# Two matmuls at once in half the array: memory attention's scores by pairs of heads, and the forget gate's 16-row products

## The chip, the cores and the metric

The kernel runs on one core of one Trainium2 chip. The metric is the device time of one execution in microseconds (us). The runs before the change gave a median of 926.34 us (three runs, 926.17 to 926.77). The profiled execution is one of its own: 927.06 us, of which the span from the first to the last instruction is 924.4.

## The reference

The model has two layers; the change is in the first. A tile of 256 tokens (`x`, 256 x 1024) goes through a wide projection, then three branches are gated and added, then a feed-forward part, then a second layer (state space and dilated attention). All is float32. The two places that the change touches are these:

```python
# the forget gate of gated linear attention: 16 columns of the projection, then a 16 x 512 matrix
log_a = log_sigmoid(a_gla @ w_gla_gate + b_gla_gate) / 16.0        # a_gla 256 x 16, w_gla_gate 16 x 512

# memory attention: 4 heads, keys of 64, values of 256; 256 tokens against 256 rows of a memory
s_m = einsum('bshd,bmhd->bhsm', q_m, k_m) * (MEM_DQK ** -0.5)       # MEM_DQK = 64
p_m = softmax(s_m, axis=-1)
o_mem = einsum('bhsm,bmhd->bshd', p_m, v_m)
```

Beside memory attention stands gated linear attention: its decayed products between tokens of a chunk are made level by level (nine levels, from the diagonal up).

## The kernel before

Each engine has its own program, written out by hand in one order, and the engines meet at semaphores. Weights stream from memory through a ring of three slots. A projection of 1024 x 1024 is a "group": seven block products of 128x512 blocks (numbered 1 to 7, in an order such as 1, 5, 2, 7, 3, 6, 4) in place of eight. Sums of weight blocks and of row blocks (`group_t1`, `t3`, `t2`, `t4`, `group_rows`) and the sums of the results (`group_z`, `group_v`, `group_last`) are made by VectorE; a full sum of weights (128x2048) is a long operation there. Product 5 waits for t1, 7 for t3, 6 for t2, 4 for t4 and z. In the text (GT,2) is product 2 of group GT. The groups around the change are MV (the memory's values), GT and GU (two gates).

A float32 matmul shows as two LDWEIGHTS and two MATMUL records.

**The forget gate.** ScalarE copies the 16 gate columns of both token tiles out of PSUM into `a_tok` (line 796). TensorE turns them (`turn("ga", ...)`), ScalarE copies the result into rows 0 to 15 of `aT`, and the job "gg" (lines 2249 to 2251) multiplies `wgate[0:16]` and `aT[0:16]` for the four heads in turn, right before the job "q2".

**Memory attention and the levels** share a stage of nine steps, i = 0 to 8 (TensorE from line 2526, ScalarE from line 927, VectorE from line 1599). In each step TensorE does, in this order: one or two or more products of a group; the scores of head i (i < 4); the transposes of the probabilities of head i - 1 (1 <= i <= 4), which wait for ScalarE's exponentials; the values of head i - 2 (2 <= i < 6); the products of level i. The scores of a head are two products of 128x256 over all 128 rows. Two heads share 128 rows (64 each), so for an even head the keys in `kmT[0]` have zeros in rows 64 to 127, and for an odd head those in `kmT[1]` have zeros in rows 0 to 63; GpSimd sets these zeros (lines 609 to 611), and ScalarE's `turned_keys` copies the keys in two pieces of 64 rows (line 717).

**What sets the order.** Scores, values, levels and the final outputs are "units". They use two PSUM banks in turn (`bank["score"]`). TensorE's `unit("score")` takes the next bank and first waits until the unit two before it has been taken out:

```python
if kind == "score" and n - 2 in BY_ACT:
    pe.wait_ge(sem("score_copied"), BY_ACT.index(n - 2) + 1)
elif n >= 2:
    pe.wait_ge(sem(kind + "_taken"), by_dve(n - 1) if kind == "score" else n - 1)
```

Scores and most levels are taken out by VectorE (a head by two reductions with the maximum, line 1473, called from line 1620 on), values and the levels 1, 2 and 8 by ScalarE. `linear_units` (line 84) lists the order: S0 L0 S1 L1 S2 V0 L2 S3 V1 L3 V2 L4 V3 L5 and so on. Before it takes the scores of step 0, VectorE makes `group_t1(GT)`; in step 2 it makes `group_t4(GT)` and `group_z(GT)` first. Before VectorE multiplies the operands of level 2 it waits until TensorE is done with level 1 (`if i in (1, 2, 8)`), since they use the same buffers.

All elementwise operations of VectorE between two tensors show as line 1176, all products of groups as line 2382 or 2378, all jobs as line 2297.

Of the kernel before, what the change touches and what calls it, by code (L numbers as in the profile page):

```python
# [83 lines left out]
def linear_units():  # L84

    units = []
    for i in range(9):
        units += [("scores", i)] * (i < EH) + [("values", i - 2)] * (2 <= i < EH + 2) + [("level", i)]
    return units + [("out", n) for n in range(4)]
# [68 lines left out]
for _job in JOBS:  # L158
# [43 lines left out]
    "kpe_rows": "rotated key, twice", "key_zero": "GpSimd: zeros beside the rotated key, then beside the memory's keys", "q_rows": "queries without rotation", "qpe_rows": "rotated queries",  # L202
# [69 lines left out]
def build(nc, d, out):  # L272
    with ExitStack() as ctx:
# [23 lines left out]
        a_tok = sb("a_tok", [P, TT * GR])  # L297
# [37 lines left out]
        kmT, qmT = (qpT[:, 0:512], kpeT), qpT[:, 512:1024]  # L335
# [19 lines left out]
        adiag = a1(256)  # L355
# [157 lines left out]
        def _(sp):  # L513
            def constants_of_rows():
# [9 lines left out]
                sp.dma_start(wgate[0:GR, :], d["w_gla_gate"][0]).then_inc(sem("consts_in"), 16)  # L524
# [46 lines left out]
        def _(pool):  # L571
# [9 lines left out]
            for name in list(COLS)[1:]:  # L581
                a, n = COLS[name]
                pool.dma_start(prow[a:a + n, :], d[name].rearrange("o (a b) -> (o a) b", b=P)).then_inc(sem("rows_in"), 16)
            pool.memset(kpeT[64:128, 0:SEQ], 0.0).then_inc(sem("key_zero"), 1)
# [21 lines left out]
            for n, i in enumerate(GATES):  # L606
                if n == 2:
                    pool.wait_ge(sem("mla_scores"), MH)
                    pool.memset(kmT[0][64:128, :], 0.0).then_inc(sem("key_zero"), 1)
                    pool.memset(kmT[1][0:64, 0:SEQ], 0.0).then_inc(sem("key_zero"), 1)  # L610
                    pool.wait_ge(sem("key_zero"), 4)
                    pool.wait_ge(sem("group_product"), product_at(MV, 6))
                    pool.memset(amat, 0.0).then_inc(sem("amat_zero"), 1)
# [51 lines left out]
        def _(act):  # L665
# [124 lines left out]
            ck = ckv.rearrange("p (t c) -> p t c", c=RANK + ROPE)  # L790
            for t in range(TT):
# [4 lines left out]
                act.activation(a_tok[:, GR * t:GR * t + GR], p[:, 512 * t + RANK + ROPE:512 * t + FIRST], ACT.Copy, scale=root)  # L796
# [18 lines left out]
            turned(aT[0:GR, :], SEQ, rows=GR)  # L815
# [78 lines left out]
            for t in range(TT):  # L894
                if t:
                    turned(qmT, 512)
                    turned_keys(kmT, 512)
                    act.wait_ge(sem("silu_done"), t)
# [28 lines left out]
            for i in range(9):  # L927
# [17 lines left out]
                if 1 <= i <= EH:  # L945
                    turned(softT[:, 512 * ((i - 1) % 2):512 * ((i - 1) % 2) + 512], 512)
                if i < EH:
                    exps("mem", i, ((0, 256, 0), (256, 256, 1)))
                if 2 <= i < EH + 2:
# [6 lines left out]
                    ins.then_inc(sem("score_copied"), 1)  # L956
                if i == 4:
# [188 lines left out]
        def _(dve):  # L1146
# [209 lines left out]
            dve.wait_ge(sem("consts_in"), 16 * (8 + len(GAINS)))  # L1356
# [242 lines left out]
            for i in range(9):  # L1599
# [20 lines left out]
                if i < EH:  # L1620
                    p = scored()
                    s = soft[:, 512 * (i % 2):512 * (i % 2) + 512]
                    c = 340 + 2 * (i % 4)
                    zero = bc(masks[:, 0, 0:1], [P, 256])
                    link(scores(s, i, ((p[:, 0:256], s[:, 0:256], zero, c),), EQ ** -0.5, None))
                    taken_score(scores(s, i, ((p[:, 256:512], s[:, 256:512], zero, c + 1),), EQ ** -0.5, None))
                    minus(i, "mem")
                if 2 <= i < EH + 2:
# [3 lines left out]
                    mark(dve.reciprocal(st[:, 360 + 2 * h:362 + 2 * h], st[:, 350 + 2 * h:352 + 2 * h]), "mem_sum")  # L1632
                    h, (_, _, z, v), biased = group(GT)[0], temporaries(GT), ckv[:, 0:512]
# [581 lines left out]
        def _(pe):  # L2215
# [28 lines left out]
            def matmuls(name, half):  # L2244
# [4 lines left out]
                if o == "gg":  # L2249
                    return [(p[:, SEQ * h:SEQ * h + SEQ], wgate[0:GR, P * h:P * h + P], aT[0:GR, :], True, True)  # L2250
                            for h in (2 * half, 2 * half + 1)]
# [178 lines left out]
            turn("ga", [a_tok[:, GR * t:GR * t + GR] for t in range(TT)])  # L2430
# [13 lines left out]
            pe.wait_ge(sem("consts_in"), 16 * (8 + len(GAINS)))  # L2444
# [76 lines left out]
            pe.wait_ge(sem("key_zero"), 4)  # L2521

            vm3 = vm.rearrange("p (t c) -> p t c", c=DM)
            vg3 = vg.rearrange("p (t c) -> p t c", c=DM)

            for i in range(9):
# [6 lines left out]
                if i < EH:  # L2533
                    b = unit("score")
                    for t in range(TT):
                        ins = pe.matmul(b[:, SEQ * t:SEQ * t + SEQ], qmT[:, SEQ * (i // 2) + P * t:SEQ * (i // 2) + P * t + P],
                                        kmT[i % 2][:, SEQ * (i // 2):SEQ * (i // 2) + SEQ], start=True, stop=True)
                    ins.then_inc(sem("score_ready"), 1)
                if 1 <= i <= EH:
                    pe.wait_ge(sem("mem_exp"), i)  # L2540
                    s = soft[:, 512 * ((i - 1) % 2):512 * ((i - 1) % 2) + 512]
                    turn(f"mem{i - 1}", [s[:, P * k:P * k + P] for k in range(4)])
                if 2 <= i < EH + 2:
# [10 lines left out]
                    ins.then_inc(sem("score_ready"), 1)  # L2554
                if i:
# [395 lines left out]
```

## Time and profile before

| | us |
|---|---|
| median of the runs | 926.34 |
| the profiled execution | 927.06 |
| its span | 924.4 |
| TensorE busy | 917.3 (99%) |
| VectorE busy | 721.6 (78%) |
| ScalarE busy | 241.1 (26%) |
| GpSimd busy | 46.0 (5%) |

The busy time of an engine is the sum of the time in which it shows an instruction. Matmuls are pipelined, so TensorE's busy time says little of how fast it goes; its granted clock was 1.00 of 2.4 GHz in all the stretches looked at here. The chain that ended last is followed back from the last instruction, at each step to what released it. A time in brackets behind a line of the timeline is the idle time of the engine before it, and who ended it.

### The profile page before, as it was taken

The numbers are of one execution on the slowest core, as the hardware profiler recorded it, in microseconds if no ns is written. First come the engines' busy times: TensorE is split into PE (matmuls) and PEld (weight loads), VectorE is DVE, ScalarE is ACT, GpSimd is POOL, SyncE is SP. The second block draws the span as 40 slices with busy tenths as digits, with TensorE's granted clock in tenths as the row PEclk, the third lists the DMA queues.
The fourth block names the chain that finished last, engine by engine and source line by source line (L and its number), as shares of the span: only waits on it lengthen the run. The fifth ranks groups of instructions, "written<-read, shape, count | busy, mean of one in ns | idle before, by whom it ended". The sixth has DMA issues, their size and how long they took to land.

```text
span 924.4 us, 12502 instructions
## 1 busy us (share of the span) xinstructions
PE 917.3 (99%) x4961; PEld 580.9 (63%) x4961; DVE 721.6 (78%) x1208; ACT 241.1 (26%) x469; POOL 46.0 (5%) x74
## 2 busy tenths in 40 slices
PE   9999999999999999999999999999999999999998
PEld 7944555945645459999744459547864444469444
DVE  5885965589899677958899855888999898575686
ACT  2415422233433322332100011311212222534210
POOL 2400000000006300000000001000000000000000
PEclk9999999999999999999999999999999999999999
DMA  9854331553509534435555427532434434331721
GB/s 318 270 183 143 131 136 46 183 182 97 200 20 255 184 113 160 149 126 183 182 183 182 174 103 233 177 134 92 157 118 182 156 133 167 111 117 47 272 91 45
DMA packets 48201, 141.78 MB, mean 153 GB/s; under 512 B 3618, under 2 KB 7616, under 8 KB 47888
## 3 DMA queue, kind: packets, MB, share of 16 engines
q1 hardware_dynamic: 45024, 134.48, 41.4%
q0 software_dynamic: 2560, 5.93, 2.8%
q8 instruction: 39, 0.64, 0.3%
q10 hardware_dynamic: 560, 0.59, 0.2%
q14 instruction: 18, 0.15, 0.0%
HBM read 138.89 MB, written 2.10 MB: 153 GB/s over the span
## 4 chain that ended last, share of the span: by engine, by line
PE 97%; DVE 2%; ACT 0%; issue 0%; DVEq 0%; ACTq 0%
PE pair L2382 33%; PE pair L2297 26%; PE pair L2378 16%; PE pair L2660 6%; PE turned L2236 4%; PE score L2660 3%; PE turned L2660 1%; DVE arena L1176 1%; PE score L2753 1%; PE score L2496 1%; PE score L2497 1%; PE score L2552 1%; PE score L2390 1%; PE score L2820 1%; DVE ring L1176 0%; PE turned L2740 0%
## 5 line engine op out<-in xcount | busy, mean ns | idle before, releaser
L1176 DVE TENSOR_TENSOR arena<-arena 128x256 f32<-128x256 f32 (+5 forms) x348 | 194.7, 577 | 16.4 <-PE score L2660 4.1
L2297 PE MATMUL pair<-ring,hT 128*128 128x512 f32 (+1 forms) x288 | 120.2, 572 | 0.0
L2382 PE MATMUL pair<-ring,hT 128*128 128x512 f32 x256 | 116.1, 596 | 0.6 <-DVE arena L1176 0.5
L2382 PE MATMUL pair<-ring,arena 128*128 128x512 f32 x256 | 114.7, 594 | 0.0
L2382 PE MATMUL pair<-arena 128*128 128x512 f32 x208 | 93.9, 593 | 0.0
L2297 PEld LDWEIGHTS pair<-ring,hT 128*128 128x128 f32 x288 | 53.6, 190 | 57.2 <-issue 55.9
L1176 DVE TENSOR_TENSOR arena<-pair,arena 128x512 f32<-128x512 f32 x66 | 46.4, 703 | 51.4 <-PE pair L2382 25.3
L2382 PEld LDWEIGHTS pair<-ring,arena 128*128 128x128 f32 x256 | 47.5, 190 | 54.3 <-issue 54.0
L2382 PEld LDWEIGHTS pair<-ring,hT 128*128 128x128 f32 x256 | 47.1, 190 | 52.8 <-issue 51.8
L1176 DVE TENSOR_TENSOR arena<-ring 128x2048 f32<-128x2048 f32 (+1 forms) x41 | 76.9, 1875 | 2.4 <-DMA ring<-in_w_ssm_out 1.0
L2297 PE MATMUL pair<-hT,ring 128*128 128x128 f32 (+1 forms) x448 | 72.6, 322 | 0.2 <-ACT hT L731 0.2
L2297 PEld LDWEIGHTS pair<-hT,ring 128*128 128x128 f32 x448 | 64.6, 191 | 6.8 <-ACT hT L731 1.0
L2382 PEld LDWEIGHTS pair<-arena 128*128 128x128 f32 x208 | 38.8, 190 | 45.1 <-issue 44.9
L2378 PE MATMUL pair<-arena 128*128 128x128 f32 x544 | 64.2, 276 | 0.0
L2378 PEld LDWEIGHTS pair<-arena 128*128 128x128 f32 x544 | 62.2, 192 | 0.3
L2378 PE MATMUL pair<-hT,ring 128*128 128x128 f32 x480 | 55.9, 276 | 0.0
L2378 PEld LDWEIGHTS pair<-hT,ring 128*128 128x128 f32 x480 | 54.7, 192 | 0.6 <-issue 0.5
L1176 DVE TENSOR_TENSOR arena<-arena,ring 128x2048 f32<-128x2048 f32 (+1 forms) x26 | 51.1, 1964 | 1.8 <-PE pair L2378 0.7
L2236 PEld LDWEIGHTS turned<-ident,arena 128*128 128x128 f32 (+1 forms) x323 | 37.8, 141 | 16.4 <-issue 13.8
L748 ACT ACTIVATE arena<-pair 128x512 f32<-128x512 f32 x38 | 22.6, 597 | 93.0 <-PE pair L2382 64.8
L1176 DVE TENSOR_TENSOR ring<-ring 128x2048 f32<-128x2048 f32 (+1 forms) x23 | 44.2, 1921 | 2.5 <-PE pair L2382 1.1
L2297 PE MATMUL pair<-ring,arena 128*128 128x512 f32 (+2 forms) x128 | 44.6, 503 | 0.7 <-DVE arena L1176 0.7
(285 smaller groups left out, 1066.3 us busy)
## 6 DMA issues: line engine op xcount, KB each, us to landing
ring<-in_w_in SPq DMA_DIRECT2D x33, 2048.0 KB, 8.4
ring<-in_w_up SPq DMA_DIRECT2D x8, 2048.0 KB, 8.7
ring<-in_w_down SPq DMA_DIRECT2D x8, 2048.0 KB, 8.3
ring<-in_w_o SPq DMA_DIRECT2D x4, 2048.0 KB, 8.0
ring<-in_w_mem_kv SPq DMA_DIRECT2D x2, 2048.0 KB, 7.9
ring<-in_w_glu SPq DMA_DIRECT2D x2, 2048.0 KB, 8.7
ring<-in_w_ssm_out SPq DMA_DIRECT2D x2, 2048.0 KB, 8.0
ring<-in_w_ukv SPq DMA_DIRECT2D x1, 2048.0 KB, 9.1
```

The source lines that it names most:

```text
L748: act.activation(temporaries(i)[q == 5], group(i)[0][1 if q == 1 else 3], ACT.Copy).then_inc(sem("group_act"), 1)
L1176: return dve.tensor_tensor(o, a, b, op)
L2236: ins = pe.transpose(b[0:x.shape[1], a:a + rows], x, ident[0:rows, 0:rows])
L2297: ins = pe.matmul(o_, s, m, start=a, stop=b)
L2378: ins = pe.matmul(h[bank_][:, P * c:P * c + P], weights[:, k, P * c:P * c + P], rows[:, k, :], start=not onto and c == 0 and k == 0, stop= ...
L2382: ins = pe.matmul(h[bank_], rows[:, k, :], weights[:, k, :], start=not onto and k == 0, stop=k == 3, skip_group_check=True)
L2390: pe.matmul(bank["score"][0][:, 0:P], ones, ones, start=True, stop=True)
L2496: pe.matmul(o, qnT[:, SEQ * h + P * t:SEQ * h + P * t + P], knT[:, SEQ * h:SEQ * h + w], start=True, stop=False)
L2497: ins = pe.matmul(o, qpT[:, SEQ * (h // 2) + P * t:SEQ * (h // 2) + P * t + P], kpeT[:, SEQ * (h % 2):SEQ * (h % 2) + w], start=False, sto ...
L2552: ins = pe.matmul(b[:, SEQ * t:SEQ * t + SEQ], s[:, 256 * t + P * k:256 * t + P * k + P], vm3[:, k, EV * h:EV * h + EV], start=k == 0, sto ...
L2660: ins = pe.matmul(product[q], rows[:, k, :], weights[:, k, :], start=g == 0 and k == 0, stop=g == 7 and k == 1, skip_group_check=True)
L2753: ins = pe.matmul(b[:, 256 * h + P * i:256 * h + P * i + P], bt[r, 2048 * i + P * n:2048 * i + P * n + P], u2[r, CH * n:CH * n + CH], star ...
```

## The change

The heads of memory attention are taken in pairs. In steps 0 and 2 the scores of two heads (0 and 1, then 2 and 3) are made, each as products over its own 64 rows, in the order (tile 0, head even), (tile 0, head odd), (tile 1, even), (tile 1, odd), each head into its own bank. So two matmuls stand in different halves of the array's rows. The zeros and the two copies of the keys fall away. The transposes of heads 0 and 1 stand in step 1, of head 2 in step 3 ahead of the values of head 1, of head 3 in step 3 behind them. Values stay in steps 2 to 5. The order of units is S0 S1 L0 L1 S2 S3 V0 L2 V1 L3 V2 L4 V3 L5.

The forget gate's 16 columns are kept twice, in columns 0 to 15 and 64 to 79 of a tile of 128 columns of zeros (GpSimd writes the zeros, in a place that is used later by the levels), the gate's weights are loaded twice (rows 0 to 15 and 64 to 79), and each half of the job takes head 0 or 1 from the lower and head 2 or 3 from the upper rows.

```diff
@@ linear_units
-        units += [("scores", i)] * (i < EH) + [("values", i - 2)] * (2 <= i < EH + 2) + [("level", i)]
+        units += [("scores", h) for h in (i, i + 1) if i in (0, 2)] + [("values", i - 2)] * (2 <= i < EH + 2) + [("level", i)]
@@ buffers
-        a_tok = sb("a_tok", [P, TT * GR])
-        kmT, qmT = (qpT[:, 0:512], kpeT), qpT[:, 512:1024]
+        kmT, qmT = qpT[:, 0:512], qpT[:, 512:1024]
-        adiag = a1(256)
+        adiag = a1(256); a_tok = adiag
@@ SP: constants
-                sp.dma_start(wgate[0:GR, :], d["w_gla_gate"][0]).then_inc(sem("consts_in"), 16)
+                for q in (0, 64):
+                    sp.dma_start(wgate[q:q + GR, :], d["w_gla_gate"][0]).then_inc(sem("consts_in"), 16)
@@ GpSimd
+            pool.memset(a_tok, 0.0).then_inc(sem("a_zero"), 1)
+            pool.wait_ge(sem("a_zero"), 1)
             pool.memset(kpeT[64:128, 0:SEQ], 0.0).then_inc(sem("key_zero"), 1)
...
                 if n == 2:
-                    pool.wait_ge(sem("mla_scores"), MH)
-                    pool.memset(kmT[0][64:128, :], 0.0).then_inc(sem("key_zero"), 1)
-                    pool.memset(kmT[1][0:64, 0:SEQ], 0.0).then_inc(sem("key_zero"), 1)
-                    pool.wait_ge(sem("key_zero"), 4)
@@ ScalarE
+            act.wait_ge(sem("a_zero"), 1)
-                act.activation(a_tok[:, GR * t:GR * t + GR], p[:, 512 * t + RANK + ROPE:512 * t + FIRST], ACT.Copy, scale=root)
+                for q in (0, 64):
+                    act.activation(a_tok[:, P * t + q:P * t + q + GR], p[:, 512 * t + RANK + ROPE:512 * t + FIRST], ACT.Copy, scale=root)
-            turned(aT[0:GR, :], SEQ, rows=GR)
+            turned(aT[:, :], SEQ)
-                    turned_keys(kmT, 512)
+                    turned(kmT, 512)
@@ ScalarE, the stage's steps
-                if 1 <= i <= EH:
-                    turned(softT[:, 512 * ((i - 1) % 2):512 * ((i - 1) % 2) + 512], 512)
-                if i < EH:
-                    exps("mem", i, ((0, 256, 0), (256, 256, 1)))
+                if i == 1:
+                    for e in range(2):
+                        turned(softT[:, 512 * e:512 * e + 512], 512)
+                if i == 3:
+                    turned(softT[:, 0:512], 512)
+                if i in (0, 2):
+                    for h in (i, i + 1):
+                        exps("mem", h, ((0, 256, 0), (256, 256, 1)))
...  (the values of head i - 2 are copied here, as before)
+                if i == 3:
+                    turned(softT[:, 512:1024], 512)
@@ VectorE, the stage's steps
-                if i < EH:
-                    p = scored()
...
+                if i in (0, 2):
+                    for h in (i, i + 1):
+                        p = scored()
+                        s = soft[:, 512 * (h % 2):512 * (h % 2) + 512]
+                        c = 340 + 2 * (h % 4)
+                        zero = bc(masks[:, 0, 0:1], [P, 256])
+                        link(scores(s, h, ((p[:, 0:256], s[:, 0:256], zero, c),), EQ ** -0.5, None))
+                        taken_score(scores(s, h, ((p[:, 256:512], s[:, 256:512], zero, c + 1),), EQ ** -0.5, None))
+                        minus(h, "mem")
@@ TensorE, the job gg
-                    return [(p[:, SEQ * h:SEQ * h + SEQ], wgate[0:GR, P * h:P * h + P], aT[0:GR, :], True, True)
-                            for h in (2 * half, 2 * half + 1)]
+                    return [(p[:, SEQ * h:SEQ * h + SEQ], wgate[32 * h - 32 * half:32 * h - 32 * half + GR, P * h:P * h + P],
+                             aT[32 * h - 32 * half:32 * h - 32 * half + GR, :], True, True) for h in (half, half + 2)]
@@ TensorE, the gate's transposes
-            turn("ga", [a_tok[:, GR * t:GR * t + GR] for t in range(TT)])
+            turn("ga", [a_tok[:, P * t:P * t + P] for t in range(TT)])
@@ TensorE, the stage's steps
-                if i < EH:
-                    b = unit("score")
+                if i in (0, 2):
+                    two = [unit("score") for _ in range(2)]
                     for t in range(TT):
-                        ins = pe.matmul(b[:, SEQ * t:SEQ * t + SEQ], qmT[:, SEQ * (i // 2) + P * t:SEQ * (i // 2) + P * t + P],
-                                        kmT[i % 2][:, SEQ * (i // 2):SEQ * (i // 2) + SEQ], start=True, stop=True)
-                    ins.then_inc(sem("score_ready"), 1)
-                if 1 <= i <= EH:
-                    pe.wait_ge(sem("mem_exp"), i)
-                    s = soft[:, 512 * ((i - 1) % 2):512 * ((i - 1) % 2) + 512]
-                    turn(f"mem{i - 1}", [s[:, P * k:P * k + P] for k in range(4)])
+                        for e, b in enumerate(two):
+                            r = slice(64 * e, 64 * e + 64)
+                            ins = pe.matmul(b[:, SEQ * t:SEQ * t + SEQ], qmT[r, SEQ * (i // 2) + P * t:SEQ * (i // 2) + P * t + P],
+                                            kmT[r, SEQ * (i // 2):SEQ * (i // 2) + SEQ], start=True, stop=True)
+                            if t:
+                                ins.then_inc(sem("score_ready"), 1)
+                for h in {1: (0, 1), 3: (2,)}.get(i, ()):
+                    turn_probabilities(h)
...
+                if i == 3:
+                    turn_probabilities(3)
```

The waits on `consts_in` count one transfer more, TensorE's wait for GpSimd's zeros beside the memory's keys is gone, and `turn_probabilities(h)` is the old wait and transposes of a head as a function.

## Rows read from the trace of the kernel before

**Rows 1.** The page: busy time by engine, and the chain's shares by engine.
```profile
PE 917.3 (99%) x4961; PEld 580.9 (63%) x4961; DVE 721.6 (78%) x1208; ACT 241.1 (26%) x469; POOL 46.0 (5%) x74
...
PE 97%; DVE 2%; ACT 0%; issue 0%; DVEq 0%; ACTq 0%
```

**Rows 2.** The chain of waits in order of time: start us, us, engine and line.
```profile
71.66 29.58 PE pair L2297 x72
...
214.32 0.86 PE score L2536 x4
...
233.80 1.73 PE score L2552 x8
...
260.61 2.30 DVE ring L1176
...
275.55 3.67 PE pair L2382 x8
```

**Rows 3.** Waits of VectorE, then of TensorE, 214 to 276: total us, times, longest.
```profile
DVE arena L1176 <- PE score L2568: 2.2, 2, 1.3
DVE ring L1176 <- PE pair L2382: 1.1, 1, 1.1
PE pair L2382 <- DVE arena L1176: 0.5, 1, 0.5
```

**Rows 4.** Timelines of TensorE and VectorE, 71 to 90: start us, us, [idle before, releaser].
```profile
71.59 1.99 PE L2297 MATMUL pair<-arena 16*128 16x256 f32 x8
73.51 14.00 PE L2297 MATMUL pair<-ring,hT 128*128 128x512 f32 x32
...
80.90 1.23 DVE L1420 SCALAR_TENSOR_TENSOR arena<-arena 128x1024 f32<-128x1024 f32 x1 [3.17 <-ACT arena L830]
...
89.53 0.55 DVE L1408 TENSOR_REDUCE stats<-arena 128x3 f32<-128x384 f32 x1 [3.73 <-ACT arena L834]
```

**Rows 5.** The chain again: pairs over 64 rows, and full records of 128x128.
```profile
579.84 1.09 PE score L2753 x16
...
350.40 28.59 PE pair L2378 x256
```

**Rows 6.** Last gain's DMA (us to landing), ScalarE and TensorE around the gate's operands.
```profile
gains<-in_k_norm_w SPq DMA_DIRECT2D x1, 96.0 KB, 8.0
...
27.60 2.17 ACT L735 ACTIVATE arena<-turned,pcol 128x128 f32<-128x128 f32 x8 [1.61 <-PE turned L2236]
...
50.01 0.38 PE L2236 MATMUL turned<-ident,a_tok 128*16 128x128 f32 x2
```

**Rows 7.** Timeline of VectorE, 206 to 276.
```profile
206.48 1.23 DVE L1176 TENSOR_TENSOR arena<-arena 128x1024 f32<-128x1024 f32 x1 [2.11 <-ACT arena L899]
...
207.74 1.42 DVE L1176 TENSOR_TENSOR arena<-pair,arena 128x512 f32<-128x512 f32 x2
...
214.27 2.29 DVE L1176 TENSOR_TENSOR arena<-ring 128x2048 f32<-128x2048 f32 x1
...
217.06 0.42 DVE L1473 CUSTOM_DVE_ANT_0 arena<-score,masks 128x256 f32<-128x256 f32 x1
...
221.69 2.29 DVE L1176 TENSOR_TENSOR ring<-ring 128x2048 f32<-128x2048 f32 x1
...
233.32 0.69 DVE L1176 TENSOR_TENSOR arena<-arena,pair 128x512 f32<-128x512 f32 x1
...
274.71 0.69 DVE L1176 TENSOR_TENSOR arena<-arena,pair 128x512 f32<-128x512 f32 x1
```

**Rows 8.** Timeline of ScalarE: the copies of the turned keys.
```profile
204.11 1.18 ACT L717 ACTIVATE arena<-turned 64x512 f32<-64x512 f32 x2
```

**Rows 9.** Timeline of TensorE, 215 to 233.
```profile
215.12 0.76 PE L2568 MATMUL score<-arena 128*32 128x32 f32 x64
...
223.76 0.60 PE L2236 MATMUL turned<-ident,arena 128*128 128x128 f32 x4
...
232.34 1.03 PE L2536 MATMUL score<-arena 128*128 128x256 f32 x4
```

More of the change, by code:

```diff
@@ L201 @@
     "x_rows": "normalised tiles of x", "mem_rows": "normalised tiles of the memory", "ckv_rows": "tiles of the latent",
-    "kpe_rows": "rotated key, twice", "key_zero": "GpSimd: zeros beside the rotated key, then beside the memory's keys", "q_rows": "queries without rotation", "qpe_rows": "rotated queries",
+    "kpe_rows": "rotated key, twice", "a_zero": "GpSimd: zeros around the forget gate's columns", "key_zero": "GpSimd: zeros beside the rotated key", "q_rows": "queries without rotation", "qpe_rows": "rotated queries",
     "k_rows": "keys without rotation", "m_rows": "memory attention's queries, then keys",
@@ L1354, in _ @@
             group_t2(0)
-            dve.wait_ge(sem("consts_in"), 16 * (8 + len(GAINS)))
+            dve.wait_ge(sem("consts_in"), 16 * (9 + len(GAINS)))
             link(dve.tensor_copy(posf[:, :], posi[:, :]))
@@ L1619, in _ @@
                     group_last(GT, gt4[2])
-                if i < EH:
-                    p = scored()
[L1622 to L1627, printed above, removed]
+                if i in (0, 2):
[7 more added lines that the diff above has]
+                        minus(h, "mem")
                 if 2 <= i < EH + 2:
@@ L1632, in _ @@
                     mark(dve.reciprocal(st[:, 360 + 2 * h:362 + 2 * h], st[:, 350 + 2 * h:352 + 2 * h]), "mem_sum")
+                if i in (0, 2) or 2 <= i < EH + 2:
                     h, (_, _, z, v), biased = group(GT)[0], temporaries(GT), ckv[:, 0:512]
@@ L2443, in _ @@
             is_turned("ga")
-            pe.wait_ge(sem("consts_in"), 16 * (8 + len(GAINS)))
+            pe.wait_ge(sem("consts_in"), 16 * (9 + len(GAINS)))
             job("gg")
@@ L2520, in _, with turn_probabilities @@
             is_turned("km")
-            pe.wait_ge(sem("key_zero"), 4)
             vm3 = vm.rearrange("p (t c) -> p t c", c=DM)
             vg3 = vg.rearrange("p (t c) -> p t c", c=DM)
+            def turn_probabilities(h):
+                pe.wait_ge(sem("mem_exp"), h + 1)
+                s = soft[:, 512 * (h % 2):512 * (h % 2) + 512]
+                turn(f"mem{h}", [s[:, P * k:P * k + P] for k in range(4)])
             for i in range(9):
```

## Prediction, before the result was known

> **What bounds the kernel now.** I read the page first: TensorE is busy for 99% of the span, VectorE for 78%, and 97% of the chain that ended last runs over TensorE [rows 1]. So almost any TensorE time that goes away could be span, and any new wait of TensorE is span at once. Next the chain of waits in order of time: from 71.66 to 101.24 it is a single stretch of TensorE, which begins with the forget gate's job; the same holds around memory attention up to 260.5; then, from 260.61 to 275.4, it leaves TensorE and runs over VectorE, and TensorE comes back with product 4 of group GU at 275.55 [rows 2]. Then the timelines of VectorE, TensorE and ScalarE over 203 to 276, because the change reorders these 60 us. The reader is to see that VectorE is nearly full there: between 214 and 276 it idles for 3.3 us in all, each time waiting for TensorE (2.2 for level products, 1.1 for product 5 of GU), while TensorE waits for VectorE only once, 0.5 us [rows 3].
>
> Names: S, V, L are the "scores", "values" and "level" units, numbered by head or level; step i is the loop index of the stage. "Shift" is how much later than before something happens. I work out the stage without the gate's saving and subtract that at the end.
>
> **The gate's job.** Its eight records take 71.59 to 73.51, of which the eight matmuls are 8 x 0.215 = 1.72 (a 128x256 record costs 0.86/4 = 0.215 in the chain) [rows 2, 4]. Twice two heads now sit in rows 0 to 15 and 64 to 79 and write different banks. The rows for such pairs are the state space job's: 16 records of 64x128 take 1.09, against 16 x 28.59/256 = 1.79 for full records of 128x128 [rows 5]. Eight pair slots at the full record's 0.112 would be 0.89, so a pair costs what one costs and the block has 0.20 of its own at its edges. With 16 rows no pair is shown: the saving lies between 0 and 0.86. I take 0.86, since the shown pairs reach the ideal rate, and since the edge is paid today too (1.92 against 1.72). Does it reach the end? VectorE waits 1.23 for this job and 3.17 and 3.73 further on for ScalarE, which follows q2; TensorE runs through [rows 4]. VectorE then works without a gap until 116.9, all of it counted from q2's end, so it moves along. **-0.86.**
>
> *Edges by the Trainium skill.* The row shows 0.20 per block. The Trainium skill's "TensorEngine Tiling (Array Packing)", section "Key Properties", says that changing the tiling mode drains the engine; the trace agrees in kind, the page gives no price. Its "Theoretical Speedup" of up to 2x taken bare would make the sum below 0.2 lower, for the one edge that shows in it.
>
> **Preparing the gate's operands.** The second weight DMA costs SP another 0.58 before the gains and the next weights (24.41); VectorE takes the constants at 34.45 without idling, the last gain is issued at 23.94 and takes 8.0 [rows 6], so 31.9 becomes 32.5; g1x is wanted by VectorE at 45.44. ScalarE copies 16 columns four times, +0.15 to 0.3 each, then product 1's copy at 25.35, with 1.61 idle behind it. GpSimd's zeros stand before 7 us, wanted at 22.7. The transposes of 128x128 cost what those of 16 columns do (0.11) [rows 6]. All 0; if the DMA's cover went, 0.6.
>
> **Step 0 of the stage: the new wait.** The banks "score" are two, and a unit waits until the unit two before it has been taken out. Before, S0 and L0 followed units long gone. Now S0, S1, L0 are neighbours, so L0 waits for S0, which VectorE evicts. VectorE is late there: it is on group_t1(GT) from 214.27, and takes S0 at 216.59 and 217.06 (+0.42 = 217.48) [rows 7]. TensorE would have S0, S1 ready at 214.32 + 4 x 0.215 + 0.20 = 215.4. A small gain comes first: ScalarE copies the memory's keys in one piece instead of two (1.18 for two, so 0.58 less), and its sigmoid at 205.32 is what VectorE waits for until 206.48 [rows 7, 8]; but VectorE then needs product 6 of MV (TensorE, about 207.6) instead of starting at 207.74, so only 0.15 of it counts. S0 is out at 217.33, and from VectorE's end to TensorE's start is 0.15 (275.40 to 275.55) [rows 2, 3]: L0 starts at 217.48 instead of 215.12 [rows 9]. Behind L0 in TensorE's order stand (GT,2), (GT,5) and all else. **Shift +2.36**, and the pair's own speed is worthless here: it ends 2 us before the eviction.
>
> **Step 1.** S1 is gone (0.86), a second head's transposes are added (0.44) [rows 9]: -0.43, **shift +1.93**. VectorE has S1's 1.14 earlier; t3(GT), which (GT,7) needs, ends at 225.1, and (GT,7) starts at 227.3, so covered. VectorE must wait for L1 before it overwrites the operands: start 227.3 instead of 225.89, so z(GT), which ended at 234.0, ends near 235.4 [rows 7].
>
> **Step 2: a second wait.** (GT,3) ends at 232.34 + 1.93 = 234.27; S2 and S3 take 1.06; VectorE can start S2 at about 235.55 (TensorE's end plus 0.1), needs 0.89, and V0 (two units after S2) starts 0.15 later, at 236.6. Before, V0 began 1.30 after (GT,3), behind one score block and one transpose; now 2.33 [rows 2, 9]. L2 waits for S3, evicted during V0's 1.73: hidden. +1.03, **shift +2.96**.
>
> **Steps 3 and 4.** S3's 0.86 gone and 0.44 of transposes added, then 0.44 of transposes gone: -0.43 and -0.44, **shift +2.1**. No other bank wait appears: V0 is copied by ScalarE long before V1 has to give way, L3 to L8 keep their distances.
>
> **The end of the stage.** (GU,5) ends 2.1 late. VectorE's t2(GU) at 260.61 had waited 1.14 for it [rows 3]; VectorE's own work before it hangs on L3 (shift 2.5) and would be ready at 262.0, before 262.7. From there to z(GU) and (GU,4) VectorE runs without a gap, so (GU,4) starts at 277.65: the whole 2.1 stays. Behind it both engines go on together and nothing in the chain is anchored elsewhere. GpSimd's two memsets less and its wait less are off the path. **+2.1.**
>
> *Eviction by the Trainium skill.* What the row shows is an eviction of 0.89 per head by VectorE [rows 7]. The Trainium skill's "TensorEngine Tiling (Array Packing)", section "PSUM Bottleneck", warns that tiling speeds TensorE and not the copying out of PSUM. By it alone, with VectorE free as soon as S0 is there, the sum would be 1.0 lower; the trace goes further, since VectorE first finishes 2.3 us of weight sums.
>
> **Sum.** +2.1 - 0.86 = +1.24. The profiled execution took 927.06 (span 924.4 and 2.7 around it), 0.7 above the median of 926.34; the difference goes onto either: 928.30, or 927.6 on the median. That is 0.13%, within the 0.2% (1.85 us) that a measurement of this kernel can tell from no change.
>
> **Rivals.**
> *A: the waits are hidden.* If VectorE got to S0 and S2 in time, the stage would give 3.44 - 2 x 1.06 = 1.3 less 0.2 for the edge loads behind them, and the gate 0.86: 924.4. For it: VectorE's three idles add up to 3.3, enough to follow. Against it: VectorE's row at 214.27 stands directly before S0. Chance 0.12.
> *B: 16-row products do not overlap, slower.* Place: the gate's job; price: 0.86 not gained, total +2.1: 928.4. It decides once the starts of its records lie 0.2 apart instead of in twos. For it: no row shows pairs of fewer than 64 rows. Against it: level products in four column groups of 32 do run at once (64 records in 0.76 [rows 9]). Chance 0.14.
> *C: longer waits, slower.* Place: step 2, where S2 and z(GT) finish within 0.2 us of each other. If L1 or z(GT) comes over 0.2 later than I have it, each further 0.1 delays V0 by 0.1; if the 64-row score pairs do not overlap either, +0.66. 928.2 to 929.1. Chance 0.12.
> The forecast itself: 0.62.
>
> **Numbers.** Faster: most of A, since its 924.4 is just past the bound at 924.5, and a little of the forecast, 0.09. Slower, above 928.2: most of B and C, and the upper edge of the forecast, 0.26. Same: 0.65. Range 925.2 to 929.0: down to where half of A is in, up to C's end.
>
> **What would show it.** Right: in the gate's job starts in twos and about 1.06 from first to last end; TensorE idle for some 2 us before the first L2568 group, released by VectorE, and some 0.9 before the first values of step 2; VectorE waiting over 1 us for L1; (GU,4) 1.2 later than 275.55 with the gate's saving in. Wrong: no idle before L0 (A); (GU,4) at 275 or earlier; the stretch from the gate to the first query transposes unchanged at 29.6 (B).

## The result, and the profile after

The changed kernel took 929.10 us (median of 7 executions, 928.01 to 930.45) beside 926.65 for the kernel before (7 executions, 926.17 to 927.12): ratio 1.0026, 95% interval 1.0016 to 1.0035. It is slower by 0.26%, and 0.1 us above the range of 925.2 to 929.0. Measured again beside other kernels, it took 928.45 (11 executions, 927.20 to 929.96), before 926.86, ratio 1.0016 (1.0008 to 1.0025). One thing is needed to understand these numbers: the changed kernel's executions fall into two groups by span, 925.4 to 925.9 and 926.7 to 927.6, and 10 of these 18 are in the upper one; the kernel before has two groups of its own, 923.9 to 924.9 and, in 17 of 76 executions beside the experiments, 925.4 to 926.2, which a late last transfer would explain (last section). The time around the span varies too, from 1.8 to 3.6 in whatever kernel. The profiled execution (930.06, span 927.6) is in the upper group. Before's profiled span was 924.4.

The page of the changed kernel answers to [rows 1]: the engines' busy time is the same, but the chain has moved 2% of its span from TensorE to VectorE.

```profile
span 927.6 us, 12504 instructions
...
PE 917.2 (99%) x4961; PEld 579.1 (62%) x4961; DVE 721.7 (78%) x1208; ACT 240.5 (26%) x470; POOL 44.5 (5%) x73
...
PE 95%; DVE 4%; ACT 0%; issue 0%; DVEq 0%; ACTq 0%
```

The chain of waits in order of time (start us, us, engine and line) answers to [rows 2]. TensorE's stretch from the gate's job on is 28.73 where it was 29.58. Then, at 213.52, the chain leaves TensorE for VectorE: a weight sum of 2.30 and the two evictions of S0, and only then L0 at 216.80. In step 2 it does so again, before V0 at 237.58. (GU,4) starts at 278.70, before at 275.55.

```profile
71.95 28.73 PE pair L2305 x72
...
213.52 2.30 DVE arena L1182
215.84 0.42 DVE arena L1479
216.31 0.42 DVE arena L1479
216.80 0.76 PE score L2584 x50
217.56 8.76 PE pair L2390 x16
...
236.54 0.42 DVE arena L1479
237.01 0.42 DVE arena L1479
237.58 1.97 PE score L2566 x8
...
278.70 1.52 PE pair L2390 x3
```

TensorE's timeline (start us, us, engine and line, out<-in, count, [idle before, releaser]) answers to [rows 4] and [rows 9]. The gate's block takes 1.13 where it took 1.99. L0 comes behind an idle of 1.98. And what the prediction did not have: the eight products (GT,2) behind L0 take 5.40, and the next eight of the same shape 3.60.

```profile
71.88 1.13 PE L2305 MATMUL pair<-arena 16*128 16x256 f32 x8
72.94 1.55 PE L2305 MATMUL pair<-ring,hT 128*128 128x512 f32 x3
...
213.68 1.14 PE L2551 MATMUL score<-arena 64*128 64x256 f32 x8
216.80 0.76 PE L2584 MATMUL score<-arena 128*32 128x32 f32 x64 [1.98 <-DVE stats L1479]
217.49 5.40 PE L2390 MATMUL pair<-ring,hT 128*128 128x512 f32 x8
222.72 3.60 PE L2390 MATMUL pair<-arena 128*128 128x512 f32 x8
```

The reason is in the table by stretches (us, TensorE busy and instructions, granted clock, DMA share, GB/s), first of the kernel before, then of the changed one. After 214.0 to 216.5, in which TensorE is busy 0.82 of 2.50, the granted clock of the next stretch is 0.53 of full, nearly all of it at 1.2 GHz; it is 0.97 in the stretch behind. Before, TensorE was busy throughout and the clock stayed at 1.00. (Behind the last product of the program the clock falls as well: it is at half over the last 0.3 us of the span before, and over the last 2.1 in one experiment, heads in turn. That costs nothing, but it enters the mean clock of an execution.)

```profile
214.00:216.50 2.50, 2.42 (x71) 1.00 1.01 383
217.60:221.00 3.40, 3.40 (x9) 1.00 0.21 82
```

```profile
206.00:210.00 4.00, 4.00 (x11) 1.00 0.11 45
210.00:214.00 4.00, 4.00 (x11) 1.00 0.63 173
214.00:216.50 2.50, 0.82 (x8) 1.00 1.00 387
217.60:221.00 3.40, 3.40 (x5) 0.53 0.04 14
221.00:225.00 4.00, 4.00 (x11) 0.97 0.01 2
```

TensorE's waits for VectorE in the stage (total us, times, longest): the last line is the wait that [rows 3] had, the two above it are new.

```profile
PE score L2584 <- DVE stats L1479: 2.0, 1, 2.0
...
PE score L2566 <- DVE stats L1479: 1.2, 1, 1.2
...
PE pair L2390 <- DVE arena L1182: 0.6, 1, 0.6
```

### The profile page after: what moved, and what is told of

Same layout as the page of the kernel before. It is cut to its first block, busy times and chain, and to the rows that moved or that the text cites. A ratio compares the mean times of both kernels' runs of the same rounds, so it can differ in the third digit from the quotient of the medians.

```text
span 927.6 us, 12504 instructions
## 1 busy us (share of the span) xinstructions
PE 917.2 (99%) x4961; PEld 579.1 (62%) x4961; DVE 721.7 (78%) x1208; ACT 240.5 (26%) x470; POOL 44.5 (5%) x73
## 4 chain that ended last, share of the span: by engine, by line
PE 95%; DVE 4%; ACT 0%; issue 0%; DVEq 0%; ACTq 0%
PE pair L2390 31%; PE pair L2305 25%; PE pair L2386 16%; PE pair L2676 6%; PE turned L2244 4%; PE score L2676 3%; DVE arena L1182 3%; PE turned L2676 1%; PE score L2769 1%; DVE ring L1182 1%; PE score L2566 1%; PE score L2398 1%; PE score L2504 1%; PE score L2505 1%; PE score L2836 1%; PE turned L2756 0%
```

## The experiments

"The stage" is the time from the start of S0's products to the start of (GU,4) in the profiled execution, 275.55 - 214.16 = 61.39 before and 278.70 - 213.68 = 65.02 after. It is the better measure: from the start of (GU,4) to the end of its last product TensorE needs 645.0 in all these kernels, and from q2's start to S0's 140.65 to 140.75, while the start of the gate's job alone lies anywhere from 71.0 to 71.9. The changed kernel's profiled span is 3.2 longer than before's: 3.63 from the stage, less 0.86 from the gate, and the rest, 0.4, mostly because that job started 0.3 later. T below is my theory: the new wait of L0 costs what the prediction says, and behind it the clock falls in some executions, which costs another 1.7. The kernels of the table ran in several sets, each beside the kernel before; "0.998" counts the executions whose mean granted clock was 0.998 or less. It is a hint of a fall and no proof: a late end lowers the mean too, 3 of 76 executions of the kernel before show it, and so do 3 of 11 of the gate alone, in which nothing new is waited for.

| kernel | median us | before | ratio (95%) | stage | 0.998 |
|---|---|---|---|---|---|
| changed | 929.10 | 926.65 | 1.0026 (1.0016-1.0035) | 65.02 | 4 of 7 |
| changed again | 928.45 | 926.86 | 1.0016 (1.0008-1.0025) | 64.95 | 4 of 11 |
| pairs alone | 929.47 | 926.55 | 1.0032 (1.0019-1.0044) | 63.32 | 2 of 5 |
| gate alone | 926.45 | 926.55 | 0.9996 (0.9988-1.0005) | 61.40 | 3 of 11 |
| wait alone | 930.25 | 926.55 | 1.0036 (1.0023-1.0048) | 63.72 | 2 of 5 |
| wait filled | 928.24 | 926.55 | 1.0015 (1.0006-1.0024) | 63.32 | 0 of 11 |
| scores first | 928.38 | 926.61 | 1.0014 (1.0006-1.0023) | 63.22 | 0 of 11 |
| level later | 926.45 | 926.61 | 0.9996 (0.9987-1.0005) | 61.78 | 0 of 11 |
| heads in turn | 929.35 | 926.61 | 1.0028 (1.0016-1.0039) | 63.33 | 4 of 6 |
| both moved | 925.42 | 926.61 | 0.9983 (0.9975-0.9992) | 60.48 | 1 of 11 |
| moved, full array | 925.80 | 926.86 | 0.9987 (0.9978-0.9995) | 61.22 | 0 of 11 |
| order, full array | 929.08 | 926.86 | 1.0019 (1.0011-1.0028) | 63.86 | 1 of 11 |
| longer wait | 933.02 | 926.86 | 1.0055 (1.0041-1.0069) | 67.99 | 5 of 5 |

**Each half alone.** The pairs without the gate:

```diff
-                for q in (0, 64):
-                    sp.dma_start(wgate[q:q + GR, :], ...)
+                sp.dma_start(wgate[0:GR, :], ...)
...
-                    return [(..., wgate[32 * h - 32 * half:...], aT[...], True, True) for h in (half, half + 2)]
+                    return [(..., wgate[0:GR, P * h:P * h + P], aT[0:GR, :], True, True)
+                            for h in (2 * half, 2 * half + 1)]
```

> Memory attention's heads in pairs as in the changed kernel, the forget gate as in the kernel before. Theory T: the stage of memory attention costs +2.1 by the waits of the first level and of the first values for VectorE, and in those executions in which TensorE's clock falls to 1.2 GHz behind the 2.3 us idle another 1.7: 928.8 without, 930.4 with the fall; the profile has L0 start 2.2 to 2.4 later than before. Rival R1 (the extra over the forecast comes from the gate's part, its second transfer or its 16-row pairs): 928.7 in all executions and no stretch at half clock. Rival R2 (the clock falls because half of the array works, not because of the idle) says as T here.

The gate without the pairs (memory attention as before):

```diff
-                if i in (0, 2):
-                    two = [unit("score") for _ in range(2)]
+                if i < EH:
+                    b = unit("score")
```

> The forget gate's products in two row groups, memory attention as in the kernel before. Theory T: -0.86, 925.8, all of it in the gate's job and carried to the end, clock at full in all stretches. Rival R1: no gain or a loss, 926.7 or more. Rival R3 (the gain is lost further on, since VectorE's or the DMAs' order does not move along): 926.6.

All of the loss is in the pairs: alone they have it, and the gate alone has none. In its profile TensorE's chain from the gate's job is 28.73, as in the changed kernel, and the stage is 61.40, as before; the span is 923.6, 0.8 less.

```profile
71.74 28.73 PE pair L2301 x72
```

Its median is only 0.1 under before's, because 6 of its 11 executions have longer spans (924.4 to 925.3) than the other five (923.5 to 923.7); none of the six was profiled, so the reason is open. The profile of the pairs alone has the idle of 1.98 before L0 but no slow products behind it (3.70 for eight), and its stage is 63.32, 1.9 more than before.

**The wait alone.** The kernel before, with one wait added: TensorE starts L0 only when head 0's scores have been taken out.

```diff
+                if i == 0:
+                    pe.wait_ge(sem("score_taken"), by_dve(LINEAR["scores", 0] + 1))
                 b = unit("score")
```

> The kernel before with one more wait and nothing else: before the products of level 0 TensorE waits until head 0's scores are out of PSUM. All products use the whole array. Theory T: L0 2.5 later than before, nothing gives it back (VectorE's later waits are all for TensorE): 929.1 with the clock at full, and 930.8 where it falls to 1.2 GHz behind the idle. Rival R2: the clock never falls here, 929.1. Rival R4 (the slack of VectorE gives part of the wait back): 928.0 or less.

TensorE's timeline: an idle of 2.37, and the stage 2.33 longer.

```profile
214.41 1.03 PE L2536 MATMUL score<-arena 128*128 128x256 f32 x4
217.81 0.76 PE L2570 MATMUL score<-arena 128*32 128x32 f32 x64 [2.37 <-DVE stats L1473]
```

Nothing of the change is in this kernel but the wait, and it is at least as slow as the changed one (which also has the gate's saving). In this profile the clock stayed at 1.00, so the wait's own price can be read: its idle, and nothing of it comes back. Its span of 928.6 has another 1.6 from a late last transfer (last section). Two of its five executions have a mean clock of 0.998, but no profile shows a fall behind full-array products.

**The wait filled.** Two useless products of 128x512 with TensorE's operands at hand, put between S1 and L0 of the changed kernel; the wait itself stays.

```diff
+                if i == 0:
+                    for _n in range(2):
+                        pe.matmul(bank["turned"][n_unit["turned"] % 2][:, :], hT[:, 0, 0:P], hT[:, 0:2, :], start=True, stop=True)
```

> The changed kernel with two more 128x512 products, of no use, into a free bank between the scores of heads 0 and 1 and the level that waits (1.7 us of TensorE, within the wait of 2.3). Theory T: L0 starts when it did, the clock stays at 2.4 GHz in every execution, and the time is 928.0 to 928.2, near the executions of the changed kernel whose clock was full (928.0 and 928.4). Rival R2: half clock as often as in the changed kernel, 929.1 or more. A third view, that the wait ends with TensorE's own work and not with VectorE's eviction: 1.7 slower, 930.8.

TensorE's timeline and its table by stretches:

```profile
214.40 1.98 PE L2576 MATMUL turned<-hT 128*128 128x512 f32 x4
216.45 0.76 PE L2587 MATMUL score<-arena 128*32 128x32 f32 x64
```

```profile
214.00:217.00 3.00, 2.94 (x73) 1.00 1.01 401
217.00:221.00 4.00, 4.00 (x33) 1.00 0.07 26
```

L0 starts where it did, since VectorE releases it, but the clock stays at 1.00 and the stage is 63.32 instead of 65.02: 1.7 less. All 11 spans are 925.4 to 926.0, the changed kernel's lower group; its upper group is gone. The stage is the test of the clock's part; the groups only support it, since late ends make an upper group as well, and their share varies: 5 of 21, 11 of 28 and 1 of 27 in before's three sets, and by their spans 6 of 11 with the scores first (below), where no clock was under 0.999. The median falls little (928.24 beside 928.45), as the changed kernel's median in that later set was itself just below the border of its two groups.

**The wait made longer.** One more useless weight sum on VectorE, ahead of the one that delays S0's eviction.

```diff
+                    dve.wait_ge(sem("group_product"), product_at(MV, 4))
+                    link(tt(t2_, b11, b12, ALU.add))
```

> The changed kernel with one more 128x2048 sum of VectorE, of no use, before group_t1(GT): the idle before L0 is 4.7 instead of 2.35. Theory T: +2.3 by the idle, and the clock falls in every execution instead of in part of them, so the time is 2.3 above the slower executions of the changed kernel: 932.2, the profile with a stretch at 1.2 GHz behind the idle. Rival R6 (the stretch at half clock in the one profile of the changed kernel was chance, not due to the idle): 931.3 and no such stretch.

The stretches of the section on the profile after:

```profile
214.00:216.50 2.50, 0.64 (x6) 1.00 1.01 392
217.60:221.00 3.40, 2.05 (x66) 0.50 0.03 10
221.00:225.00 4.00, 4.00 (x7) 0.62 0.01 2
```

The idle before L0 is now 4.31, the clock is low in both later stretches, and each of the 5 executions has a mean clock of 0.996 to 0.998. An idle of 1.98 is followed by a fall in some profiles and not in others, this one by a fall in its profile and, as far as the mean clock tells, in every execution. The eight products (GT,2) take 5.72 here.

**The changed kernel again**, in the set of the last four kernels:

> The changed kernel itself once more, for its distribution beside the others of this set. Theory T: spans in two clusters, near 925.9 (clock at full) and near 927.5 (a fall behind the idle, or the last result's transfer landing 1.6 later, which the kernel before shows too in 11 of 28 executions); median 928.9. Rival R6: the upper cluster no more frequent than in the kernel before: 928.2.

```profile
217.60:221.00 3.40, 3.40 (x5) 0.57 0.02 8
```

The fall is no accident of one profile: the stage is 64.95 (65.02 in the first). But the median execution of this set, 928.45, has a span of 925.6 and a mean clock of 1.000; it is one without the fall.

**VectorE takes the scores first.** In step 0 VectorE's weight sum t1(GT) is moved behind both evictions.

```diff
-                if i == 0:
-                    group_t1(GT)
                 ... S0 and S1 are taken
+                if i == 0:
+                    group_t1(GT)
```

> The changed kernel with VectorE's sum group_t1(GT) moved behind the scores of heads 0 and 1, so that it evicts head 0 as soon as TensorE has it. Theory T (the wait before L0 is VectorE's lateness, and the idle of over 2 us is what lets the clock fall): L0 waits 1.1 instead of 2.35, the clock stays at 2.4 GHz in the profile, the wait before the first values stays at 1.1 to 1.4; stage +1.2, gate -0.86: 926.9. Rival R4 (VectorE is the bound of the whole stage, so an idle put before its sum is given back in full at (GU,4)): 928.2. Rival R2 (clock falls because half the array works): half clock here as well, 928.5.

This was a miss: 928.38 against 926.9. L0's wait did shrink to 1.10, and no execution had a mean clock of 0.998, but the time came back elsewhere (and 6 of the 11 spans, 926.6 to 927.2, lie 1.6 above the other five, as late ends would put them):

```profile
215.49 0.76 PE L2584 MATMUL score<-arena 128*32 128x32 f32 x64 [1.10 <-DVE stats L1479]
...
225.45 7.13 PE L2390 MATMUL pair<-ring,arena 128*128 128x512 f32 x16 [0.18 <-DVE ring L1182]
...
235.35 1.97 PE L2566 MATMUL score<-arena 128*128 128x256 f32 x8 [1.70 <-DVE stats L1479]
```

(GT,7) now waits for t3(GT), and V0 waits 1.70 where it waited 1.2. VectorE stood idle for 1.5 until S0 was there, and being nearly full it had that time no more in step 2. The stage is 63.22, 0.1 less than with the wait filled. Taking the one wait away from in front of VectorE's work moved it to the next.

**L0 one step later.** L0's products and its eviction are moved into step 1, so that no unit stands two behind S0 in step 0.

```diff
-                if i:
-                    pe.wait_ge(sem("level_ready"), i)
+                if i == 0:
+                    continue
+                if i == 1:
+                    ... L0's products, then L1's
```

> The changed kernel with level 0 moved on TensorE from step 0 to step 1, behind (GT,2), (GT,5) and the transposes, and VectorE's masking of it to step 1. Theory T: no wait in step 0, clock at full; the wait of the first values for head 2's eviction becomes longer, since TensorE comes earlier to it: V0 1.4 later than before, +0.6 at the end of the stage, gate -0.86: 926.3. Rival R4: as the changed kernel with the clock at full, 928.0. Rival R2: half clock, over 929.

```profile
213.37 1.13 PE L2555 MATMUL score<-arena 64*128 64x256 f32 x8
214.89 3.67 PE L2394 MATMUL pair<-ring,hT 128*128 128x512 f32 x8 [0.39 <-ACT arena L746]
...
234.02 1.97 PE L2570 MATMUL score<-arena 128*128 128x256 f32 x8 [1.26 <-DVE stats L1479]
```

The first wait is gone (0.39 is left, for a copy of ScalarE), the second stays, and the stage is 61.78: 0.4 above before. With the gate's 0.86 that is the kernel before within what can be measured.

**Heads in turn.** The scores over 64 rows as in the change, but head 1's products behind both of head 0's, to see what pairing itself is worth.

```diff
-                    for t in range(TT):
-                        for e, b in enumerate(two):
+                    for e, b in enumerate(two):
+                        for t in range(TT):
```

> The changed kernel with the four score products of a pair in the order of heads (head even tile 0, tile 1, head odd tile 0, tile 1), all still over 64 rows. Theory T: two matmuls at once give nothing here, since both pairs end before VectorE is through with its work: within 0.3 of the changed kernel, 928.9, with L0 and V0 starting as there. Rival R5 (the pair's speed does count, in step 2 at least): 0.4 to 0.9 slower than the changed kernel.

It didn't test what it was meant to. The block is as short as in pairs (1.14, and the stage 63.33, as the pairs' without a fall), so TensorE works on both row groups at once even when their products are not issued alternately. Its time, 929.35, is the changed kernel's within the intervals. Its profile has the idle of 1.98 too, and no fall; the span (927.0) has a late end.

**The order with full-array scores.** The changed order of units, but each head's scores as products over 128 rows with zeros beside the keys, as before.

```diff
-                            ins = pe.matmul(b[...], qmT[r, ...], kmT[r, ...], start=True, stop=True)
+                            ins = pe.matmul(b[...], qmT[:, ...], kmT[e][:, ...], start=True, stop=True)
```

> The changed kernel's order with the scores over all 128 rows against keys with zeros, two heads one after the other: the order of the change without its half-array products. It has the gate's pairs. Theory T: the loss comes from the order alone. Step 0's pair hides in the wait as before, step 2's is 0.5 later: 929.6, and the clock can fall behind the idle here too (the idle is 1.7 instead of 2.35). Rival R2 (half-array products are what costs): 927 or less and no fall.

```profile
213.20 1.89 PE L2555 MATMUL score<-arena 128*128 128x256 f32 x8
216.60 0.76 PE L2588 MATMUL score<-arena 128*32 128x32 f32 x64 [1.50 <-DVE stats L1483]
...
235.93 1.97 PE L2570 MATMUL score<-arena 128*128 128x256 f32 x8 [0.76 <-DVE stats L1483]
```

L0 starts 3.40 after S0, as in the wait alone, and 3.12 after it in the changed kernel. The 0.28 between them is not the products' speed: S0's eviction starts 2.44 behind S0's products here and 2.16 behind them there, since ScalarE copies the memory's keys in two pieces again (1.18) and VectorE comes that much later. The stage is 63.86, 2.5 above before. So it is the order that loses, with or without half-array products; these, with the keys' single copy, give back 0.5 (63.86 against 63.32), since most of what the two blocks save, 0.75 each, turns into waiting.

**Both waits moved away.** L0 in step 1 as above, and S2 and S3 in the middle of (GT,3), with VectorE taking them ahead of t4(GT) and z(GT). Once with the pairs, once with full-array scores:

```diff
+                    if i == 2:
+                        group_multiply(GT, 3, False, 0, 2)
                     ... S2 and S3
+                if i == 2:
+                    group_multiply(GT, 3, False, 1, 2)
```

> The kernel with level 0 moved to step 1, and besides the scores of heads 2 and 3 put into the middle of (GT,3), with VectorE taking them before t4(GT) and z(GT). Theory T: neither wait is left, the stage is 1.0 shorter than before by TensorE's own work and VectorE has 3.3 us of idle to follow it: 924.7, faster than before and than the changed kernel. Rival R4 (VectorE bounds the stage): (GU,4) no earlier than before save for the gate's 0.86, 925.7. A third view, a new wait for head 3's bank, which ScalarE has to empty of level 1: V0 as late as in the kernel with only the level moved, 926.3.

> The kernel with both places moved (level 0 in step 1, the scores of heads 2 and 3 inside (GT,3)), but the scores over all 128 rows against keys with zeros, as in the kernel before, so that no two run at once. It has the gate's pairs. Theory T: without a wait in the way the pairs' speed is span, two blocks of 1.72 instead of 0.86 and their edges of 0.2 to 0.3: 1.1 slower than with half-array pairs (925.4), 926.5. Rival R4 (VectorE bounds the stage): no difference, 925.4.

With the pairs it takes 925.42, ratio 0.9983 (0.9975 to 0.9992): this version beats both kernels. Its stage is 60.48, 0.9 under before's. In its chain S2 and S3 stand between two halves of (GT,3) and V0 follows without a wait:

```profile
229.46 1.06 PE score L2557 x8
230.52 1.91 PE pair L2394 x4
232.44 1.73 PE score L2574 x8
...
273.32 3.67 PE pair L2394 x8
```

TensorE has two waits left in the stage, the one of [rows 3] and one of 0.4 before (GT,2) for ScalarE's copy:

```profile
PE pair L2394 <- DVE arena L1182: 0.6, 1, 0.6
...
PE pair L2394 <- ACT arena L746: 0.4, 1, 0.4
```

The full-array version has a stage of 61.22 and takes 925.80. So once no eviction is waited for, the pairs are worth 0.74 (1.1 expected: 0.4 of it is the wait for ScalarE's copy). The two kernels' ratios lie within each other's intervals; the 0.74 is read from one profile of each, not from the times.

## Why the prediction was wrong

**The gate: right.** 0.86 was forecast and 0.86 came: 1.99 to 1.13 for the block [rows 4], 29.58 to 28.73 in the chain [rows 2]. Rival B, that 16-row products don't overlap, is refuted. It reached the end unchanged: q2's start to S0's is the same 140.7 in every kernel, with and without it.

**Preparing the gate's operands: right.** Nothing waits for it: the start of the gate's job is 71.0 to 71.9 in the profiles with the gate's change, 71.5 to 71.8 in those without.

**Step 0, the wait of L0: right in place, releaser and size.** L0 was forecast 2.36 later against S0's start; it came 2.16 later (216.80 - 213.68 = 3.12, before 215.12 - 214.16 = 0.96). Of the single copy of the keys 0.15 was taken to count; it was 0.28, the difference to the order with full-array scores; and from VectorE's end (216.31 + 0.42 = 216.73) to L0 0.07 passed where 0.15 was taken. The prediction's statement that the pair's own speed is worthless there holds: VectorE sets the start of L0 in both.

**Step 2, the wait of V0: right.** Forecast was V0 2.33 behind (GT,3) and an idle of some 0.9; it came 2.32 behind (237.58 - 235.26), with an idle of 1.19. So rival C, a longer wait, did not come true. Rival A is refuted by both waits.

**The stage: right but for one missing term.** Without a fall of the clock it is 63.3 (pairs alone, wait filled), 1.9 over before; 2.1 was forecast. With the gate that gives +1.1, forecast +1.24, and the changed kernel's lower group of spans (925.4 to 925.9) stands 1.0 to 1.5 above before's 924.4. In time these eight executions have a median of 928.3. That is 0.7 above the forecast of 927.6 and inside its range: 0.3 of it is before's median, 926.65 and not 926.34 in the same measurement, and the rest lies in the time around the span, which varies by more than that.

**The step that failed** is "Step 0 of the stage: the new wait", with "Shift +2.36" as its whole price. It priced the wait at the idle of TensorE and took the products behind it at their old durations. What the runs showed in its place: in part of the executions the granted clock falls to 1.2 GHz behind that idle, and (GT,2) takes 5.40 where eight such products take 3.67 [rows 2], +1.73. That the idle does it is shown by taking it away and leaving the wait (stage 65.02 to 63.32, the upper group of spans gone) and by making it longer (a fall again, and a low mean clock in every execution). In the first measurement 5 of 7 executions were in the upper group, so the median was one of them (929.10, span 927.3), 1.5 above the forecast and 0.1 out of the range. In the later one 5 of 11 were, and the median, 928.45, was one without the fall and inside the range. So it was partly luck on which side of the upper bound the median came; the missing term is real either way. No row of before shows such an idle of TensorE inside the stage, so its cost should have been bounded from above too: by products at half clock for some time behind it, which would have put the top of the range near 930.

The Trainium skill, "TensorE: Matmul & The Clock Gate", section "HAM oscillation — how this bites in real kernels", says that TensorE drops to the lower clock when the gaps between its bursts of products are long enough. The gaps that it names are longer than the forecast's first wait, so by its rule alone the time would not have moved. The idle of 4.31 agrees with it (0.50 of the clock behind it); the idle of 1.98, with 0.53 behind it, does not, and there the measurement decides.

**What stays open.** Why the same idle tips the clock in one execution and not in the next: with 1.98 the two profiles of the changed kernel show the fall, and those of the pairs alone and of heads in turn don't; nor does that of the wait alone, with 2.37. No run here tests that. Nor is it shown how many executions of the changed kernel had the fall beyond the two profiled; the others are told by span and mean clock only, and a late end looks the same in both. Half-array products alone don't bring it (wait filled), but no profile shows it behind full-array products either.

## What to carry to other kernels

Two units moved next to each other make the second's neighbour wait for an eviction that used to be long gone: for each unit that shares two banks, ask which one is two before it and who takes it out, and what that engine does just then. Where TensorE is the bound, a wait of 2 us cost its idle here and, in part of the executions, nearly as much again in slow products behind it; fill it or move it, and price it with both. An engine that is nearly full in a stage, as VectorE here (3.3 us idle in 62, [rows 3]), gives an avoided wait back at the next place: two waits had to be moved together before the saving of 0.9 came out.

## What the runs showed of the hardware

- The clock: behind 1.98 of idle it was 0.53 in the stretch of 3.4 us that was looked at, which made eight products 1.73 longer, in 2 of the 4 profiles with this idle; behind 4.31 of idle it was 0.50 in that stretch and 0.62 in the next 4.0. With idles of 1.10 and 1.50 (scores first; order with full array) it stayed at 1.00 in both profiles, and one of 22 executions had a mean of 0.998.
- Products over two halves of the rows overlap also when all of one half are issued before the other's (heads in turn): the row below (line, engine, operation: duration ns min/median/max) has 376 ns for a score record, eight of them took 1.14 in all, as in pairs, and eight full-array records of the same size 1.89.

```profile
L2551 PE MATMUL score<-arena x16: 376/376/480, 213.2 to 233.8; 64*128 64x256 f32 x16
```

- The end of the program has two lengths: in 11 of the 14 profiles the span ends 3.8 to 3.9 behind the last product, in those of the wait alone, level later and heads in turn 5.5. In the profile of the wait alone the last products start at 919.49 and take 3.62, and the span ends 5.5 behind them (928.6 - 923.1); before, they start at 916.90 and the span ends 3.9 behind (924.4 - 920.5). The last DMA issues of the result (out<-in, queue, operation, count, KB each, median us from issue to landing) are where it shows, first with the wait alone, then before. No execution of before with a longer span was profiled; that its upper group (925.4 to 926.2) comes from this is inferred from the same 1.6. With changes of 1 us this alone can hide or feign a result; the stage's length isn't touched by it. Why the landing varies is open.

```profile
out<-xres ACTq DMA_DIRECT2D x2, 64.0 KB, 3.4
```

```profile
out<-xres ACTq DMA_DIRECT2D x2, 64.0 KB, 2.6
```
